# Silu of every c vector on 32 columns and spread by TensorE, the first modulation half on TensorE and half on VectorE, sums of squares on GpSimd, the first head's products together with the low-rank gates

## The reference, cut to what matters

```
silu_c, silu_cc = silu(c), silu(c_ctx)                    # 1024 each
mod   = split(silu_c  @ ada_w + ada_b, 6)                 # ada_w: 1024 x 6144
mod_c = split(silu_cc @ ada_w + ada_b, 6)
u     = modulate(rmsnorm(x, g),   mod[0],   mod[1])       # x: 512 tokens x 1024
u_ctx = modulate(rmsnorm(ctx, g), mod_c[0], mod_c[1])     # ctx: 256 tokens x 1024
# modulate(h, shift, scale) = h * (1 + scale) + shift
t     = u @ w_in    # low-rank gate inputs (gr), per head q, forget gates, values, ...
```

## Time and profile before

| | us |
|---|---|
| median of 3 runs (lowest, highest) | 5740.35 (5739.34, 5742.77) |
| the profiled execution: time | 5735.39 |
| the profiled execution: span | 5734.1 |
| TensorE matmul busy | 5014.3 (87%) |
| VectorE busy | 3311.0 (58%) |
| ScalarE busy | 1863.2 (32%) |
| GpSimd busy | 1038.4 (18%) |
| mean granted TensorE clock | 0.95 of full |

### The profile page before, as it was taken

How to read it: one execution, slowest core, us unless ns; L and a number is a source line. 1 busy time by engine, 2 the same in 40 slices (tenths; PEclk the granted TensorE clock), 3 DMA queues, 4 the chain that set the end, 5 groups by cost and what they waited for, 6 DMA issues and landing times.

```text
span 5734.1 us, 68095 instructions
## 1 busy us (share of the span) xinstructions
PE 5014.3 (87%) x27685; PEld 4207.6 (73%) x27685; DVE 3311.0 (58%) x5606; ACT 1863.2 (32%) x2685; POOL 1038.4 (18%) x941
## 2 busy tenths in 40 slices
PE   3999989974779999999779988889999789979998
PEld 2898877753678888888557776668888567757776
DVE  6343445669957777776555456655444554554544
ACT  1333532221833333333341323313222333332322
POOL 0111100014834445543100001000000000000000
PEclk9999989987999999999899999999999899999998
DMA  3111113411378888885103011131111101102221
GB/s 141 45 44 45 45 45 132 154 60 37 162 248 294 306 300 303 306 298 200 53 8 126 34 67 72 41 125 59 59 60 60 41 30 60 49 27 96 81 88 59
DMA packets 156839, 639.47 MB, mean 112 GB/s; under 512 B 12176, under 2 KB 62352, under 8 KB 105072
## 3 DMA queue, kind: packets, MB, share of 16 engines
q1 hardware_dynamic: 111808, 467.96, 23.0%
q0 software_dynamic: 42496, 162.96, 8.1%
q10 hardware_dynamic: 2224, 4.19, 0.2%
HBM read 598.36 MB, written 36.70 MB: 111 GB/s over the span
## 4 chain that ended last, share of the span: by engine, by line
PE 73%; DVE 15%; ACT 5%; issue 3%; DMA 2%; POOL 1%; SPq 0%; DVEq 0%; POOLq 0%; ACTq 0%
PE banks L234 61%; PE banks L2614 2%; DVE cols L2556 2%; PE banks L2649 1%; PE banks L2530 1%; PE banks L2535 1%; PE banks L292 1%; DVE prod L502 1%; PE banks L890 1%; DVE PT L2621 1%; DVE spl0L L196 1%; PE banks L339 1%; PE banks L1863 1%; DVE raw L502 1%; ACT spl0H L181 1%
## 5 line engine op out<-in xcount | busy, mean ns | idle before, releaser
L234 PE MATMUL banks<-UH,spl1H 128*128 128x512 f32 (+1 forms) x1632 | 601.2, 368 | 39.4 <-issue 14.4
L196 DVE TENSOR_TENSOR spl0L<-raw,spl0H 128x2048 fp32r<-128x2048 f32 (+3 forms) x169 | 371.6, 2199 | 389.6 <-ACT spl0H L181 351.0
L234 PE MATMUL banks<-UH,spl1L 128*128 128x512 f32 (+1 forms) x1632 | 595.1, 365 | 0.0
L234 PE MATMUL banks<-UL,spl1H 128*128 128x512 f32 (+1 forms) x1632 | 594.8, 364 | 0.0
L196 DVE TENSOR_TENSOR spl1L<-raw,spl1H 128x2048 fp32r<-128x2048 f32 (+2 forms) x168 | 378.4, 2252 | 338.1 <-ACT spl1H L181 332.1
L234 PE MATMUL banks<-UH,spl0H 128*128 128x512 f32 (+2 forms) x1152 | 420.9, 365 | 75.7 <-DVE UL L431 50.6
L181 ACT ACTIVATE spl1H<-raw 128x2048 fp32r<-128x2048 f32 (+2 forms) x168 | 313.2, 1864 | 507.7 <-PE banks L234 317.3
L181 ACT ACTIVATE spl0H<-raw 128x2048 fp32r<-128x2048 f32 (+3 forms) x169 | 305.7, 1809 | 428.5 <-PE banks L234 209.5
L234 PE MATMUL banks<-UpH,spl0H 128*128 128x384 f32 (+1 forms) x1072 | 369.7, 345 | 68.1 <-DVE spl0L L196 56.8
L234 PE MATMUL banks<-UL,spl0H 128*128 128x512 f32 (+2 forms) x1152 | 417.1, 362 | 0.0
L234 PE MATMUL banks<-UH,spl0L 128*128 128x512 f32 (+2 forms) x1152 | 416.5, 362 | 0.0
(11 more groups left out here) (453 smaller groups left out, 11700.6 us busy)
## 6 DMA issues: line engine op xcount, KB each, us to landing
raw<-uT_in SPq DMA_DIRECT2D x64, 1024.0 KB, 8.1
raw<-ev_in SPq DMA_DIRECT2D x64, 1024.0 KB, 5.3
raw<-up_in SPq DMA_DIRECT2D x44, 1024.0 KB, 4.8
raw<-ada_in SPq DMA_DIRECT2D x40, 1024.0 KB, 4.9
side<-ada_in SPq DMA_DIRECT2D x32, 1024.0 KB, 7.0
gd<-stage SPq DMA_DIRECT2D x12, 2048.0 KB, 6.9
gt<-gd SPq DMA_DIRECT2D x32, 768.0 KB, 7.3
raw<-gate_in SPq DMA_DIRECT2D x24, 1024.0 KB, 6.3
```

The lines of the kernel that those rows point to most:

```text
L196: v.e.tensor_tensor(s.l[:, 0:w], k.raw[j % RAW][:, 0:w], s.h[:, 0:w].bitcast(F32), ALU.subtract).then_inc(*v.inc("w_lo", j))
L234: ins = pe.e.matmul(out, x, y, start=start and i == 0 and j == 0, stop=stop and i == n - 1 and j == 2)
```

## The change

1. All four vectors (c, c_ctx, c_2, c_ctx_2) come as `cf`, 128 x 32, with features on partitions. Silu is taken on those 32 columns. For each pair, VectorE multiplies an identity repeated 16 times with 16 columns (`cdg`, 128 x 2048), TensorE multiplies that with ones, which leaves each value on all partitions, and ScalarE copies it from PSUM into `cs1` or `cs2`. GpSimd stores both to DRAM after its other work; the expert stage only loads `cs2`.
2. The shift half of the first modulation stays on VectorE (4 tiles, 16 multiplications); the scale half is 64 matmuls of two columns on TensorE, from 4 tiles `adan` in the other layout. All 8 tiles have a buffer of their own and are issued at the start.
3. Squares are all on ScalarE, in two buffers; GpSimd adds them up (7 additions of 128 x 768); TensorE sums once, with 6 matmuls. The masks move behind the modulation.
4. Low-rank gates, head 0's q and head 0's f are formed together, per chunk of u. Both first weight tiles are split before u is made.

```diff
-def project_together(k, outs, tile, kcs, U, ready):
+def project_together(k, outs, kcs, U, ready):
     for kk in range(kcs):
         ready(kk)
...
+        for out, tile, (c0, m), (r0, n) in outs:
+            last.append(product(k.pe, out, [(tile[:, kk, c0:c0 + m], U[:, kk, r0:r0 + n])], start=kk == 0, stop=kk == kcs - 1))
...
+NFIRST = 4
 def setup_sp(k):
     sp = k.sp
+    sp.e.dma_start(k.cf[:], k.dram["cf"]).then_inc(*sp.inc("c_in", 0, by=16))
     for t in range(NFIRST):
-        first_ada_sp(k, t)
+        sp.e.dma_start(k.first_cols[t][:], k.dram["adan"][t]).then_inc(*sp.inc(f"cols_in{t}", t, by=16))
+        sp.e.dma_start(k.first_rows[t][:], k.dram["ada"][t]).then_inc(*sp.inc(f"rows_in{t}", t, by=16))
+    fill_raw(k, 2)
     for d in range(2):
         sp.e.dma_start(k.score[d][:], k.dram["causal"][d]).then_inc(*sp.inc("causal_in", d, by=16))
...
 def setup_pool(k):
...
+    for c in range(KC):
+        square_sum(g, k.n1.s, c)
 def setup_act(k):
     a = k.act
-    a.e.dma_start(k.cb1[:], k.dram["cb"][0]).then_inc(*a.inc("cb_in", 1, by=16))
     a.e.dma_start(k.X[:, :, 0:TX], k.dram["xT"]).then_inc(*a.inc("x_in", "x", by=16))
...
+    for i, cs in enumerate((k.cs1, k.cs2)):
+        for r in range(2):
+            a.wait_ge("mm", ("c", i, r))
+            a.e.activation(cs[:, r * D:(r + 1) * D], k.W[2 * i + r], ACT.Copy).then_inc(*a.inc("silu", ("c", i, r)))
...
+def setup_pe(k):
+    pe = k.pe
+    for i in range(2):
+        pe.wait_ge("setup", ("cdg", i))
+        for j in range(16):
+            ins = pe.e.matmul(k.W[2 * i + j // 8][:, (j % 8) * 128:(j % 8 + 1) * 128], k.ones[:], k.cdg[:, j, :], start=True, stop=True)
...
 def first_pe(k):
     pe = k.pe
+    cf = k.cf[:].rearrange("p (i r c) -> p i r c", i=2, r=2)
+    for t in range(NFIRST):
+        pe.wait_ge(f"cols_in{t}", t)
+        pe.wait_ge("silu", ("c", 0, 0))
+        tile = view(k.first_cols[t][:], KC)
+        for i in range(2):
+            c = 2 * t + i
+            for kk in range(KC):
+                ins = pe.e.matmul(k.B[0][:, 2 * c:2 * c + 2], tile[:, kk, 128 * i:128 * i + 128], cf[:, 0, :, kk],
+                                  start=kk == 0, stop=kk == KC - 1)
+            ins.then_inc(*pe.inc("mm", ("first_cols", c)))
...
     norm_mod_pe(k, k.n1)
 def first_act(k):
-    stats_act(k, k.n1.s, lambda e, i: e.wait_ge("x_in", "ctx"))
+    a = k.act
+    a.wait_ge("x_in", "x")
+    a.wait_ge("x_in", "ctx")
+    for c in range(KC):
+        square_act(k, k.n1.s, c, k.X[:, c, :])
+    root_act(k, k.n1.s)
     fill_hi(k, SPL)
...
 def first_dve(k):
     v = k.dve
...
+    v.wait_ge("silu", ("c", 0, 1))
+    for t in range(NFIRST):
+        v.wait_ge(f"rows_in{t}", t)
+        dots_dve(k, k.dots1, k.first_rows[t], t, t, k.MOD[0], ("tile", t))
...
+    root_dve(k, k.n1.s)
     v.wait_ge("scale", "b1")
-    fill_lo(k, 1)
+    fill_lo(k, SPL)
     norm_mod_dve(k, k.n1)
...
 def experts_sp(k):
...
-    sp.e.dma_start(k.cb2[:], k.dram["cb"][1]).then_inc(*sp.inc("cb_in", 2, by=16))
     load_gates(k, 0)
+    sp.wait_ge("cs2", "out")
+    sp.e.dma_start(k.cb2[:], k.dram["cs2"]).then_inc(*sp.inc("cb_in", 0, by=16))
     load_side(k, 0)
...
 def experts_dve(k):
     v = k.dve
     v.after("spread", "pe", "act", "pool")
-    for r in range(2):
-        silu_dve(k, 2, r, k.cb2, k.cbt2)
+    v.wait_ge("cb_in", 0)
```

More of the change, by code:

```diff
@@ L343, with __init__ @@
 class Sums:
-    def __init__(self, k, name, n, width, sums, rows):
+    def __init__(self, k, name, n, width, sums, rows, added="sq_sum"):
         self.name, self.n, self.width, self.sums, self.rows, self.nt = name, n, width, sums, [rows], width // 128
+        self.added = added
         m = k.m
@@ L531, in setup_plan, with first_plan @@
     k.lbt = [m.sb("lbt", [128, 16]) for _ in range(3)]
+    k.cf, k.cft = m.sb("cf", [128, 32]), m.sb("cft", [128, 32])
     k.setup_top, m.top = m.top, top
+NFIRST = 4
+def first_plan(k):
+    m = k.m
+    start = m.top
+    k.U = m.pair("U", [128, KC, T])
+    top, m.top = m.top, max(start, k.setup_top)
+    tiles = [m.sb("first", [128, TW]) for _ in range(2 * NFIRST)]
+    k.first_rows, k.first_cols = tiles[:NFIRST], tiles[NFIRST:]
+    assert m.top >= top
+    k.cs1, k.cs2 = m.sb("cs", [128, 2 * D]), m.sb("cs", [128, 2 * D])
+    at = m.top
+    k.cdg = m.sb("cdg", [128, 16, 128])
+    k.dots1 = Dots(k, "first", k.cs1)
+    end, m.top = m.top, at
+    k.n1 = NormMod(k, "n1", k.X, k.sc1, k.MOD[0][:, 0:8, :], k.U, BOTH, sums_at=end, sums=6, rows=2)
+    k.n1.s.added = "sq_sum_pool"
+    m.top = top
 def setup_sp(k):
     sp = k.sp
+    sp.e.dma_start(k.cf[:], k.dram["cf"]).then_inc(*sp.inc("c_in", 0, by=16))
     for t in range(NFIRST):
-        first_ada_sp(k, t)
+        sp.e.dma_start(k.first_cols[t][:], k.dram["adan"][t]).then_inc(*sp.inc(f"cols_in{t}", t, by=16))
+        sp.e.dma_start(k.first_rows[t][:], k.dram["ada"][t]).then_inc(*sp.inc(f"rows_in{t}", t, by=16))
+    fill_raw(k, 2)
     for d in range(2):
         sp.e.dma_start(k.score[d][:], k.dram["causal"][d]).then_inc(*sp.inc("causal_in", d, by=16))
-    fill_raw(k, 1)
-    for t in range(NFIRST, 8):
-        first_ada_sp(k, t)
     fill_raw(k, SPL + RAW)
@@ L604, in setup_dve, with masks_dve @@
     v.e.tensor_scalar(k.lbs[:, 1, :], k.lbs[:, 0, :], -1.0, 1.0, ALU.mult, ALU.add).then_inc(*v.inc("setup", "lb1"))
[L607 to L625, removed]
+def masks_dve(k):
+    v = k.dve
+    for d in range(2):
+        r = k.resets[d]
+        v.e.memset(r[:], 1.0).then_inc(*v.inc("setup", ("reset", d)))
+        x0 = T - TX if d else 0
+        v.wait_ge("setup", ("reset", d))
+        v.e.memset(chunked(r[:, x0:x0 + TX])[:, :, 0:1], 0.0).then_inc(*v.inc("setup", ("starts", d)))
+        c0 = 0 if d else TX
+        v.wait_ge("setup", ("starts", d))
+        v.e.memset(r[:, c0:c0 + 1], 0.0).then_inc(*v.inc("setup", "consts"))
+    v.wait_ge("causal_in", 1)
+    for d in range(2):
+        v.e.tensor_copy(k.causal[d][:], k.score[d][:]).then_inc(*v.inc("setup", ("causal", d)))
+        v.wait_ge("setup", ("causal", d))
+        v.e.memset(k.score[d][:], 0.0).then_inc(*v.inc("setup", ("score", d)))
 def first_pe(k):
     pe = k.pe
-    pe.wait_ge("const_in", "ident")
-    pe.wait_ge("setup", "consts")
+    cf = k.cf[:].rearrange("p (i r c) -> p i r c", i=2, r=2)
[3 more added lines that the diff above has]
+        tile = view(k.first_cols[t][:], KC)
+        for i in range(2):
+            c = 2 * t + i
[3 more added lines that the diff above has]
+            ins.then_inc(*pe.inc("mm", ("first_cols", c)))
+    pe.wait_ge("silu", ("c", 1, 0))
+    pe.wait_ge("silu", ("c", 1, 1))
     norm_mod_pe(k, k.n1)
@@ L660, in first_pool @@
     g = k.pool
-    g.wait_ge("silu_c", (1, 1))
-    g.e.dma_start(k.dram["cs"], k.cb1[:]).then_inc(*g.inc("cs", "out", by=16))
+    for i, (name, cs) in enumerate((("cs", k.cs1), ("cs2", k.cs2))):
+        g.wait_ge("silu", ("c", i, 0))
+        g.wait_ge("silu", ("c", i, 1))
+        g.e.dma_start(k.dram[name], cs[:]).then_inc(*g.inc(name, "out", by=16))
 def gr_plan(k):
@@ L691, in gr_act @@
     a.wait_ge("cs", "out")
+    a.wait_ge("cs2", "out")
     turn_act(k)
@@ L1596, in peer_plan @@
     k.dots3 = Dots(k, "experts", k.cb2, k.X[:, 4:8, TX:T])
-    own = m.top
     k.own.v = [m.sb("ownv", [128, D]) for _ in range(NVB)]
-    end, m.top = m.top, own
-    k.cbt2 = m.sb("cbt", [128, 2 * D])
-    m.top = side
+    end, m.top = m.top, side
     k.ot = [m.sb("ot", [128, D]) for _ in range(3)]
@@ L2059, in experts_act @@
     a.after("spread", "pe", "dve", "pool")
-    for r in range(2):
-        silu_act(k, 2, r, k.cb2, k.cbt2)
     for n in range(NT + 1):
@@ L2943, in ready @@
                 join_context_pe(k)
-        both = project_together(k, [(B[4 + 2 * i + r][:, 0:region[1]], 128 * i, region) for i in range(2)], tile, KC, k.U, ready)
+        both = project_together(k, [(B[4 + 2 * i + r][:, 0:region[1]], tile, (128 * i, 128), region) for i in range(2)], KC, k.U, ready)
         for i in range(2):
@@ L3701, in tensor_program @@
 def tensor_program(k):
+    setup_pe(k)
     first_pe(k)
```

147 lines of the change are left out of this document (66 added, 81 removed).

## The result

The changed kernel takes 5676.67 us (median of 4 runs, 5672.52 to 5679.42), the kernel before beside it 5741.56 (5739.34 to 5744.04): a ratio of 0.9886, 95% interval 0.9869 to 0.9903, 64.9 us faster. The forecast was 5679 in a range of 5668 to 5692, with 0.97 on faster; the time lies in the range, and in the likeliest case's own 5672 to 5686. The two profiled executions are 59.9 apart (5735.39 and 5675.48).

A forecast was written before the change was run, and what follows sets the result against it. TensorE was taken as the bound, with stalls at the start and in the expert stage. Savings of 41.1 + 4.5 + 15.6 = 61.2 us from the median gave 5679 us, range 5668 to 5692.

The forecast's parts named there:

- likeliest case: Whole kernel: the prediction's own case at 5679 us, spanning 5672 to 5686, given a chance of 0.65.
- Part 1: Start of the kernel up to the first u: first `nt` at 65.5 against 106.6, 41.1 us earlier.
- they share by packets: Loads at the start: queues share the DMA engines by packets, so X ends last, at 41.3.
- the rival of the collision: Modulation at the start: GpSimd's additions and VectorE's multiplications overlap, additions wait up to 8.5 us, 5687.5 in all; chance 0.12.
- Part 2: Gates and head 0 formed together: the backward gate starts 5.0 us earlier, 4.5 after a loss of pace.
- of pace: Gates and head 0: a 3.6 us stop before the backward gate may cost up to 1.8; 0.5 taken.
- Part 3: Expert stage: VectorE's split starts at 1603.7 instead of 1619.3, 15.6 us earlier.
- The sum: Whole kernel: 41.1 + 4.5 + 15.6 = 61.2 us saved, with neither lead given back later.
- the rival of a lower clock later on: TensorE after the start: a denser start lowers the granted clock; at a mean of 0.93 the time is 5767; chance 0.03.

The follow-up runs named there:

- experiment 6: Changed kernel with the two loads of X moved from ScalarE's queue to SyncE's, behind the small load of c and ahead of the modulation tiles; 5660.23 us.
- experiment 2: Changed kernel with the gates projected by themselves ahead of head 0 and one weight tile split before the first row; 5673.99 us.
- experiment 8: Gates projected apart and one weight tile split before u, against the changed kernel with X first, additions on VectorE and stores held back; 5665.45 us.
- experiment 3: Changed kernel with the expert stage's silu of c_2 and c_ctx_2 put back ahead of VectorE's first split; 5686.37 us.
- the first set: Runs on one chip of the changed kernel, 5676.67 us, beside the kernel before, 5741.56 us, with the first four follow-up runs.
- experiment 9: The changed kernel again, unchanged, on another chip; 5669.07 us.
- experiment 1: Changed kernel with all 8 modulation tiles multiplied on VectorE and TensorE's 64 two-column products gone; 5679.36 us.

## Why the prediction held, step by step

*Part 1, 41.1; measured 41.67.* The step that carried it, "they share by packets", held: in 20 to 23 the queues moved 133 and 132 packets, but 0.96 and 0.27 MB, ctx landed at 41.1 (forecast 41.3) and the last modulation tile at 31.9 (31), and experiment 6 shows that it was the queue and not the amount of bytes. GpSimd's additions ended at 57.15 (57.6), the first `nt` came at 64.92 (65.5). Smaller terms were off and hidden. The identity landed at 7.3, not 10.7, and the sixteen products behind it took 6.25, not 7.9, so the multiplications ended at 37.6, not 42.6, which is why the rival of the collision had 5.2 us to spare and not 0.4. And TensorE's products were priced at the slower pace throughout: the 64 of two columns took 0.20 to 0.36 each, where the forecast took 0.43, and ended at 46.5, not 58.5 (last section). Had they ended where the forecast put them, they would have been last, 1.3 behind the additions.

*Part 2, 4.5; measured 3.9 between the two profiles.* Two terms of the sum were off, in opposite ways. The backward gate's first matmul stands 31.27 behind the first `nt`, and 36.80 before: 5.5 earlier, where the sum had 5.0 (the stop ahead of it was 3.2, forecast 3.6). Behind that stop, from this matmul to the second sigmoid, it is 10.30, and 8.68 before: 1.6 given back, for which the forecast took 0.5 "of pace" out of at most 1.8. The granted clock shows it (97 to 100, the first rows behind the stop, and 101 to 104):

```profile
97.00:100.00 3.00, 3.00 (x8) 0.50 0.98 336
101.00:104.00 3.00, 3.00 (x17) 1.00 0.85 270
```

Counted as the forecast counts it, behind the first `nt`, part 2 is worth 3.0 to 4.7 in experiments 2 and 8. With the split of the large tile ahead of the first row, 1.0, which the forecast had in part 1, it is worth 2.0 to 3.7 by itself.

*Part 3, 15.6; measured 15.6* at the first matmul behind the split (experiment 3). Two us more come off there for the earlier landing of a store, outside my sum. TensorE still stands still 8.1 for `cb`, where I had said some 10. A multiplication behind the split takes 1.21, no longer the 2.02 of the earlier trace rows, since GpSimd's two weighings (1554.6 and 1556.6) now lie ahead of it; the split itself, beside the second of them, takes 2.61 in place of 2.29.

*To the end.* The sum had 61.2, and the lead at 1559.85 is 61.9, but not by the sum's terms alone: 41.7, 3.9 and 15.6, then 2.0 for the store, less 1.3 that went between the second sigmoid and the expert stage. That the total came so near is in part luck. Behind that matmul the two traces take 4112.4 and 4114.3 us at a granted clock of 0.96 each, so the rival of a lower clock later on is out. (The means over the changed kernel's executions were 0.944 to 0.947, over those of the kernel before 0.942 to 0.952.) The same changed kernel in its second trace has the expert matmul at 1563.07 and takes 4102.7 behind it. So with no edit at all 3 us come and go ahead of that matmul and 12 behind it, and the distance of the medians is 64.9 in the first set and 72.8 beside experiment 9. Whether a few us of the lead are given back or added can't be told from this.

*The collision.* The Trainium skill, "SBUF — State Buffer", section "SBUF: two separate sides", says that the shared port pair is held for a whole instruction. In experiments 1 and 6 a multiplication took 2.70 to 2.84 and each pair 2.75; alone they follow one another every 1.15 to 1.26, which leaves 1.5 of waiting beside an addition of 1.80. The trace agrees up to 0.3 a pair. The prediction priced the wrong side of it: it let each addition wait up to 1.2, and they waited 0.7 (six took 15.5 in place of 11.5), while each multiplication lost 1.5, for which it had no term. In both experiments it was the multiplications that held the first `nt`.

## What to carry to other kernels

When several loads start together, count packets for each queue, not bytes alone: here a small tensor with short rows on a queue of its own landed 9 us behind eight tiles of 1 MB. Whoever takes work off an engine must look at what stood behind it in its queue; here two stores of 1 MB moved up by 34 to 40 us and cost 5 of the 6 that the edit had gained. And an edit that seems right for its own sake (additions on an idle GpSimd) is to be asked who is idle at that moment: VectorE was, and the first `nt` came 6.1 sooner with its help.

## What the runs showed of the hardware

- TensorE's granted clock fell while it was busy without a pause, with products of two columns. These are its two-column products in the changed kernel (columns: stretch, length, TensorE busy and instructions, granted clock, DMA share, GB/s; two instructions make a product):

```profile
26.00:28.00 2.00, 2.00 (x20) 1.00 1.01 399
28.00:30.00 2.00, 2.00 (x14) 0.63 0.99 391
30.00:32.00 2.00, 2.00 (x11) 0.50 1.06 402
```

  The pace of these products goes with the clock, 10 instructions a microsecond at the upper level (2.4 GHz) and 5.5 at the lower one (1.2 GHz): 0.20 and 0.36 a product. The fall came at 21 to 30 in all eleven traces that have these products, and so the 64 took between 22.2 and 25.2 us where none waited for its tile. In experiment 1, which has none of them, TensorE stood still from 23.7 on, and the clock fell at 28 to 29, where it falls in the changed kernel's first trace: working on two-column products kept it up no longer than doing nothing. The forecast's 0.43 came from one-column products; the changed kernel's take 0.45 each at a granted clock of 0.50 (six in 2.69, at 57.30).
- The granted clock in the rows is not to be trusted ahead of its first recorded change. In the changed kernel it reads 1.00 in 10 to 15, where TensorE runs 25 instructions of its 128-column products, 5 a microsecond; it runs 11 in 19 to 21, at a recorded 0.50, and 11 in 22 to 23 alone, at a recorded 1.00. In the kernel before it reads 1.00 up to 300, also where 512 columns take 0.63.
- The first matmul of u meets the lower clock in all of these runs but experiment 2. The rise comes 2.8 to 5.8 us later where TensorE then goes on without a stop, and 14 to 16 where it waits for each chunk of u (experiments 2 and 8; in the kernel before, by the matmuls' own durations).
